# Another order for the head of the mixers in a two-layer hybrid backbone kernel

## What is computed

```python
u = adaln(xs) @ w_in
pool = pool_mixer(u[..., :256])                 # windowed means, then pooled @ pool_w
ssd  = ssd_bidirectional(u[..., 256:1032])      # chunks of 128 tokens, two directions
attn = attention(u[..., 1032:])                 # 4 query heads, 2 key/value heads, rotary
xs = xs + g1 * (concat([pool, ssd, attn]) @ w_out)
xs = xs + g2 * swiglu(adaln(xs))
# inside the SSD scan
a_cs = cumsum(a); decay_states = exp(a_cs[-1] - a_cs)
states = einsum(B, decay_states, x)             # one per chunk and direction
new_states = chunk_decay @ states               # a recurrence from chunk to chunk
y = (C B^T * Lmat) x + C prev_states exp(a_cs)
```

## Time and profile before

| | us |
|---|---|
| device time, median of 3 runs | 1668.36 |
| lowest and highest run | 1665.81, 1670.21 |
| span of the profiled execution, first to last instruction | 1668.2 |
| mixer stage, first layer (end of the projection to first output matmul) | 207.9 to 351.5 |
| mixer stage, second layer | 1124.3 to 1238.3 |
| PE busy over the span | 1572.4 |

### The profile page before, as it was taken

The page is one execution under the profiler, slowest core; times in us unless marked ns, Lnnn a source line. Parts: engine busy times, 40 slices in busy tenths (PEclk is TensorE's granted clock), DMA queues, the critical chain, the costliest instruction groups (busy, mean ns, idle before and its releaser), DMA issues.

```text
span 1668.2 us, 22489 instructions
## 1 busy us (share of the span) xinstructions
PE 1572.4 (94%) x9150; PEld 1416.7 (85%) x9150; DVE 894.0 (54%) x1191; ACT 595.9 (36%) x896; POOL 162.6 (10%) x159
## 2 busy tenths in 40 slices
PE   5899978889899999999999998997889899999999
PEld 4799857689899999999999997995778688888887
DVE  1667876655674555555544367447575533333333
ACT  4633445543622112222122236254554522232222
POOL 0140135002000000000000033014202000000000
PEclk9899989999999999999999998998999999999999
DMA  8546300002353333333332122220003233333322
GB/s 324 153 157 191 91 1 1 1 26 64 102 152 126 126 126 121 114 122 123 126 126 70 48 75 81 64 77 0 1 24 92 76 89 100 94 95 97 93 78 86
DMA packets 203581, 154.76 MB, mean 93 GB/s; under 512 B 8612, under 2 KB 189676, under 8 KB 203372
## 3 DMA queue, kind: packets, MB, share of 16 engines
q1 hardware_dynamic: 202060, 148.85, 28.8%
q10 hardware_dynamic: 1440, 4.78, 0.8%
HBM read 151.52 MB, written 2.10 MB: 92 GB/s over the span
## 4 chain that ended last, share of the span: by engine, by line
PE 84%; DVE 9%; ACT 4%; issue 2%; POOL 0%; DMA 0%; SPq 0%; DVEq 0%; ACTq 0%
PE banks L1720 68%; PE banks L1839 6%; PE banks L1989 1%; PE banks L1956 1%; DVE neg_max L1527 1%; PE banks L1933 1%; PE banks L1865 1%; DVE mod_sum L1199 1%; DVE nrm L1271 1%; DVE h_lo L1265 1%; DVE w_lo L1174 1%; PE banks L1647 1%; PE banks L1970 1%; PE banks L1697 1%; PE banks L1660 1%
## 5 line engine op out<-in xcount | busy, mean ns | idle before, releaser
L1720 PE MATMUL banks<-h_hi,w_hi 128*128 128x384 f32 (+3 forms) x1296 | 389.1, 358 | 26.4 <-DVE h_lo L1265 16.5
L1174 DVE TENSOR_TENSOR w_lo<-raw,w_hi 128x1056 fp32r<-128x1056 f32 x184 | 246.1, 1338 | 312.3 <-ACT w_hi L805 311.6
L1720 PE MATMUL banks<-h_lo,w_hi 128*128 128x384 f32 (+3 forms) x1296 | 385.6, 356 | 0.0
L1720 PE MATMUL banks<-h_hi,w_lo 128*128 128x384 f32 (+3 forms) x1296 | 384.9, 355 | 0.0
L805 ACT ACTIVATE w_hi<-raw 128x1056 fp32r<-128x1056 f32 x184 | 198.3, 1078 | 246.6 <-PE banks L1720 220.2
L1720 PEld LDWEIGHTS banks<-h_hi,w_hi 128*128 128x128 f32 x1296 | 237.9, 190 | 55.7 <-issue 28.4
L1720 PEld LDWEIGHTS banks<-h_hi,w_lo 128*128 128x128 f32 x1296 | 240.0, 190 | 17.1
L1720 PEld LDWEIGHTS banks<-h_lo,w_hi 128*128 128x128 f32 x1296 | 239.6, 190 | 16.1
L1720 PE MATMUL banks<-g_hi,w_hi 128*128 128x384 f32 (+1 forms) x528 | 160.0, 357 | 0.0
L1720 PE MATMUL banks<-g_hi,w_lo 128*128 128x384 f32 (+1 forms) x528 | 159.1, 355 | 0.0
L1199 DVE SCALAR_TENSOR_TENSOR mod_sum<-mod_ring,cond,mod_sum 128x1024 f32<-128x1024 f32 x126 | 158.1, 1296 | 1.4
(11 more groups left out here) (207 smaller groups left out, 1973.9 us busy)
## 6 DMA issues: line engine op xcount, KB each, us to landing
raw<-in_w_dram SPq DMA_DIRECT2D x120, 512.0 KB, 3.9
mod_ring<-in_w_mod_dram SPq DMA_DIRECT2D x96, 512.0 KB, 4.9
raw<-in_w_in_dram SPq DMA_DIRECT2D x32, 512.0 KB, 4.8
raw<-in_w_out_dram SPq DMA_DIRECT2D x16, 512.0 KB, 4.2
raw<-in_w_dram SPq DMA_DIRECT2D x16, 384.0 KB, 3.3
x_in<-in_x_dram ACTq DMA_DIRECT2D x4, 512.0 KB, 8.1
out_dram<-x_out SPq DMA_DIRECT2D x8, 256.0 KB, 2.3
inv_n<-in_count_dram ACTq DMA_DIRECT2D x4, 400.0 KB, 3.1
```

The costliest lines, as they stand in the source:

```text
L1174: dve.tensor_tensor(w_lo[n % 2][:, :], raw[n % 4][:, :], as_f32(w_hi[n % 2][:, :]), ALU.subtract).then_inc(lo_ready, 1)
L1720: ins = pe.matmul(to(p, a, b), ws[:, w], xs(k, a, b), start=(first and q == 0), stop=(last and q == 2))
```

## The change

It rewrites the head of the event list (all that comes before the loop over units), with the waits that this needs.

```diff
@@ mixer_events @@
-            ev = [("tr", "x", 0), ("tr", "x", 1), ("tr", "b", 0), ("tr", "k", 0), ("tr", "k", 1), ("cs",), ("q23", 0),
-                  ("pool", 0), ("pool", 1), ("q23", 1), ("tr", "q", 0)]
-            ev += states[:2] + [("q23", 2)] + states[2:4] + [("q23", 3)]
-            states = states[4:]
+            ev = [("cs",), ("tr", "x", 0), ("tr", "x", 1), ("tr", "b", 0), ("rot1",), ("tr", "k", 0), ("q23", 0)]
+            ev += states[:2] + [("tr", "k", 1), ("q23", 1)] + states[2:4]
+            ev += [("pool", 0), ("pool", 1), ("q23", 2), ("tr", "q", 0)] + states[4:6] + [("q23", 3)]
+            states = states[6:]
@@ ScalarE @@
-                        act.wait_ge(pm_pe, l * INCS["pm_pe"] + 2)
-                        act.activation(mix[:, e[1], r0:T], bank_of(2 + e[1], r0, T, False),
+                        act.wait_ge(pm_pe, l * INCS["pm_pe"] + e[1] + 1)
+                        act.activation(mix[:, e[1], r0:T], bank_of(3 * e[1], r0, T, False),
@@ VectorE @@
-                    if e == ("cs",):
+                    if e == ("rot1",):
                         rotate(1)
@@ TensorE @@
+                if l == 0:
+                    mod_turn(3)
                 pe.wait_ge(tok_free, tok_count(l, 4))
...
-                        if l == 0 and e == ("tr", "x", 0):
-                            mod_turn(3)
...
-                        pe.wait_ge(mods_ready, 2 * (5 if l == 0 else DEPTH * N_MOD))
+                        pe.wait_ge(rows_ready, 4 * (5 if l == 0 else DEPTH * N_MOD))
...
+                        if e[1]:
+                            pe.wait_ge(mods_ready, 2 * (5 if l == 0 else DEPTH * N_MOD))
+                        else:
+                            pe.wait_ge(trA_out, l * INCS["trA_out"] + 4)
+                            pe.wait_ge(trB_out, l * INCS["trB_out"] + 4)
...
-                            ins = pe.matmul(bank_of(2 + e[1], a, b, False), pool_bd[l][:, e[1], :], src, start=True, stop=True)
+                            ins = pe.matmul(bank_of(3 * e[1], a, b, False), pool_bd[l][:, e[1], :], src, start=True, stop=True)
...
-                        pe.wait_ge(pm_out, l * INCS["pm_out"] + 2)
                         pe.wait_ge(xw_ready, l * INCS["xw_ready"] + n_st + 1)
...
-                        elif u:
-
+                        elif u == 0:
+                            pe.wait_ge(pm_out, l * INCS["pm_out"] + 1)
+                        else:
...
+                            pe.wait_ge(pm_out, l * INCS["pm_out"] + 2)
                             pe.wait_ge(st_ready, l * INCS["st_ready"] + n_st)
```

## The result

The change makes the kernel slower: 1675.91 us (median of 4 runs, 1675.04 to 1677.35) against 1667.09 (4 runs, 1665.75 to 1670.21). The ratio is 1.0047, with a 95% interval of 1.0033 to 1.0062 (a ratio is computed from all runs and isn't exactly that of the two medians). The prediction was 1667.8 with a range of 1661 to 1672, so both the time and the side are missed.

A forecast was written before the change was run, and what follows sets the result against it. PE's dense matmuls fill most of the kernel; the mixer head was taken as latency-bound. Layers of -1.8 to 0.0 and -0.4 to +1.0 gave -2.2 to +1.0, middle -0.6 us: median 1667.8 us, range 1661 to 1672.

The forecast's parts named there:

- part 1: Head up to unit 1's maximum: by itself later, scaling +1.1 us per layer, first-layer maximum 234.8 to 236.6 against 235.52.
- part 3: First to last `ssd_y`: 0 in the first layer, -0.8 us in the second, a query transpose moving behind the last `ssd_y`.
- part 4: Behind the last `ssd_y`: one more unit and shifted query transposes; +0.65, -0.25, +2.74 us first layer, +0.45, +3.3 second.
- The table load: ACT's load, now ahead of `x_tok`: 1.28 us without the skill's extra 1.38 us drain, which would make the sum +2.2.
- Part 1, the scaling at +1.1: Head: the scaling of 12 blocks ends at about 222.3 instead of 221.16, +1.1 us in each layer.
- Rival 2: Head: POOL and DVE obstruct each other, sine products over 4.4 instead of 2.47 us; +6.0, so 1674.4 us; chance 0.08.
- Part 1, unit 1's maximum at 234.8 to 236.6: Head, first layer: bounds with PE at 2.4 and 1.2 GHz, against 235.52 before.
- Part 2, 7.1 and 7.9 us from unit 1 to `ssd_y`: Unit 1's maximum to first `ssd_y`, first and second layer, where 11.27 and 11.03 us stood: the gain.
- Part 4, 2.74 + 0.65 - 0.25 in the first layer: Behind the last `ssd_y`: added unit 2.74 us, shifted query transposes +0.65, `mix` copy no longer ahead of the gates' root -0.25.
- 3.3 + 0.45 in the second: Behind the second layer's last `ssd_y`: added unit 3.3 us with PE as the bound, shifted query transposes +0.45.
- Rival 1: Added unit behind the scan is free, TensorE stays at 2.4 GHz: -8.2 us, so 1660.2; chance 0.17.
- signs of being wrong: First layer: unit 1's maximum before 233 or after 238, or the stage's end over 4 us from 351.5.

The follow-up runs named there:

- kernel 1: The changed kernel with the scan starting in turn 2 again, as before, keeping the new head and banks: 1672.41 us, ratio to the kernel before 1.0033.
- kernel 4: The changed kernel with the cumulative sums, and ACT's table load with them, moved behind `rotate(1)`: 1674.61 us, ratio to the kernel before 1.0042.
- kernel 11: kernel 4 with the scan starting in turn 2, as before the change: 1669.93 us, ratio to the kernel before 1.0007.
- kernel 5: The changed kernel with extra matmuls, read by nobody, in PE's idle stretches in the head: 1673.2 us, ratio to the kernel before 1.0033.
- Kernel 3: The changed kernel with the next head's query transposes one turn earlier: 1672.98 us, ratio to the kernel before 1.0031.
- Kernel 2: The kernel before with six states instead of four ahead of the second unit's scores, so the scan starts in turn 1: 1675.59 us, ratio 1.0045.
- kernel 9: Kernel 2 with extra matmuls ahead of the first unit's probability transposes and the first `ssd_y`: 1672.56 us, ratio to the kernel before 1.0023.
- kernel 6: The kernel before with seven extra matmuls ahead of the seventh state: 1670.9 us, ratio 1.0017.
- kernel 7: The kernel before with extra matmuls ahead of unit 11's probability transposes (first layer) and each output projection: 1666.86 us, ratio 0.9989.
- kernel 8: The kernel before with only the pooling products' new banks and the waits that go with them, old order: 1670.05 us, ratio 1.0003.
- kernel 12: kernel 11 with kernel 7's extra matmuls at the end: 1668.75 us, ratio to the kernel before 1.0003.

## Why the prediction was wrong

By its own parts, in us of the profiled span; the middle of its sum was -0.6, and the terms below add +7.9 to it, which gives the +7.3 measured: first `ssd_y` +2.0 and +1.55 (part 1), part 3 +0.3 and +2.2, part 4 -0.4 and +1.3, outside the stages +0.9.

- **The table load.** Right. It took 1.28 us, and the next activation began 0.02 behind its end. The drain that the Trainium skill ("ScalarE: Activation LUTs", section "What ACT_TABLE_LOAD costs") adds to a switch isn't seen in the new place either.
- **Part 1, the scaling at +1.1.** Mis-sized: +1.8 and +2.0 in this profile, +1.3 and +1.3 in kernel 1 with the same code. `rotate(1)` and the first `x_w` were costed each by its own duration. Side by side DVE's second instruction takes 1.52 us instead of 1.22, in kernel 1 too, and the pair 3.00 instead of 1.18. The other 0.5 and 0.6 us are the second key transposes at half clock, behind that pair in PE's order. Rival 2 named the mechanism but put it at the sine product, where 2.77 instead of 2.47 came out, far below its deciding 4.4. The Trainium skill, "SBUF — State Buffer", section "SBUF: two separate sides", calls the port pair of the two an exclusive lock for a whole instruction. The rows agree that one stands while the other works (3.00 instead of 1.18, and 1.52 instead of 1.22 on DVE's side); I had taken its warning for the sine product alone. On the path this collision was worth about 0.3 us a layer in kernel 1, an estimate from DVE's longer second instruction. Kernels 4 and 11 don't price it, since they move the table load as well.
- **Part 1, unit 1's maximum at 234.8 to 236.6.** It came at 237.62, 1.9 us behind the middle (in the second layer too, measured from `qk_sq`). 0.75 to 0.9 is from the scaling. The rest I put down to the clock: the bounds gave half clock 1.8 us from the last states on, but in the first layer it fell already at the states ahead of unit 0, 3.16 us of idle PE before them, and in the second layer it was still down at unit 1's scores (1150 to 1155, 0.51). PE's timeline at the first of these places:

```profile
226.71 2.08 PE L1914 MATMUL banks<-x_w,b_tok 128*128 128x256 f32 x4 [3.16 <-POOL x_w L744]
```

Kernels 1 and 5 have the same head, unfilled and filled. In the first layer their unit 1 is at 28.8 and 27.5 against 29.3 here, which supports the clock. In the second it is at 25.5 and 26.5 against 27.8, and the forecast's middle, counted from `qk_sq` too, was 25.95: there the 1.9 us aren't a price of the new order but the place at which the clock's step fell in this execution. (My bounds for the second layer, -0.2 to +1.2 about the old place, also aren't those of the first, -0.7 to +1.1, and the prediction gives no reason.)
- **Part 2, 7.1 and 7.9 us from unit 1 to `ssd_y`.** Right: 7.20 and 7.58. The first `ssd_y` came 2.0 and 1.55 us behind the middle of my bounds, measured from `qk_sq`, all of it from part 1.
- **Part 3, 0 and -0.8.** Wrong by +0.3 and +2.2. Of the 2.2, 1.6 is the first `ssd_y` itself at half clock (4.16 for 2.57). The prediction took the cycle's length from places where PE was at 2.4 GHz. It didn't ask what the shift does to PE's load: in turn 2 no attention unit's product with the values stands in the list yet, PE idles, and the clock falls on the path. The -0.8 was ascribed to a query transpose. But the last cycle is as long as before, 9.9 us (10.0), without one: there the chain goes over ACT's `e_cum` and `e_in` (1186.01, 1186.60), work of the scan itself, so there was nothing to gain.
- **Part 4, 2.74 + 0.65 - 0.25 in the first layer.** Right but for 0.4: the tail grew by 2.7.
- **Part 4, 3.3 + 0.45 in the second.** Too little: +5.0. By the maxima of the units behind the last `ssd_y`, counted from it in both kernels: the unit itself cost 3.6 (3.2 to its maximum, 0.3 behind it), the `mix` copy that left ACT's chain in the first layer entered it in the second (0.6 at 1197.77, overlooked), and the third and fourth query transposes cost 0.4 each. Ahead of the fourth PE had stood still for 3.6 us, until DVE was done with the gates, and it began its last 27 us with the clock down. Kernel 3 takes 1.4 of the 5.0 away.
- **What was left out, +0.9**, is outside the stages. I have no experiment on it; it is within what one execution differs from another.

The step that failed, then, is the sum of the parts as separate prices, read from rows of the old order with PE mostly at full clock. The gain ahead of the scan was set at 3.1 to 4.9 and 1.95 to 3.35 us and came out at 2.0 and 1.1. Part 3 was set at 0 and -0.8 and was +0.3 and +1.4, above all because the shift puts the first `ssd_y` where PE has idled and the clock is down. Part 4 in the second layer was set at 3.75 and was 5.0, half of the miss being the overlooked `mix` copy. Kernel 2 shows the shift alone as a loss of 0.0045, and kernel 9, with turn 2 filled, as one of 0.0023 (its fill included): what is paid behind the scan (2.8 and 5.0 us there) outweighs the earlier start (2.9 and 3.2), and the idle PE adds about as much again. Rival 1 assumed the reverse (clock full, unit free), and neither half held.

Neither of the prediction's own signs of being wrong came: unit 1's maximum at 237.62 lies before 238, and the first stage's end at 352.56 within 4 us of 351.5. Both look at the first layer, and most of the loss was in the second.

What stays open: how much of the 7.3 us each layer's clock accounts for, and why head and shift don't add. Kernel 5 keeps the head's clock up, but its ratio can't be told from the change's, and its extra matmuls take PE time as well. The sums' early place wasn't tested with the table load and `x_w` apart.

## What to carry to other kernels

To start a chain earlier by moving independent work behind it gains only what that work doesn't cost at the end; price the end first, with its clock, since there nothing lies beside it. When an order moves, ask for each pair of DVE and POOL instructions that newly run side by side whether both read SBUF, and who waits in order behind the slower one. When a chain moves to a place with less PE work beside it, cost its matmuls at half clock, not by the rows of the old place. And when an experiment moves one event, look which start moved first before naming a cause: kernel 4 was built for the pair of `x_w`, and its rows show that `rotate(1)` moved.

## What the runs showed of the hardware

- The same 32 small matmuls took 2.57 us at 2.4 GHz and 4.16 with the clock down, behind waits in which PE did little. In the head the clock's step falls at different places from one execution to the next: the same code has unit 1 of the second layer at 25.5 with a clock of 1.00 (kernel 1) and at 27.8 with 0.50 (the changed kernel).
- Extra matmuls helped in a wait where PE was still at 2.4 GHz (kernel 9: ratio 1.0023 for 1.0045), and cost where the clock had already fallen (kernel 6: 1.0017). There they ran at half clock. At the end of a stage it is less clear: 0.9989 in kernel 7, whose clock there is also 1.00 in kernel 8 without them, and no difference that shows between kernels 11 and 12.
- POOL's two `x_w` beside DVE's rotation took 3.00 us instead of 1.18, DVE's second instruction 1.52 instead of 1.22: both sides pay, POOL more.
